# GpSimd's queue brings the second page of every pair for all eight value units of a decoder step

## The reference, cut to what matters

```python
g = x_sample                                          # (8, 4, 1024)
k_past = gather_pages(cache_k[l], page_table)         # 8 samples x 8 pages of (128, 8 heads, 64)
v_past = gather_pages(cache_v[l], page_table)
y_ssd, new_conv, new_ssm = ssd_branch(z, xbc, dt_raw, conv_state, ssm_state, ...)
    # ... y = y * silu(z); y = rmsnorm(y, norm_w)
y_att = moba_attention(q, k_all, v_all, q_start, p['rel_bias'])
h = h + jnp.concatenate([y_ssd, y_att], axis=-1) @ p['w_out'][l]
h = h + cross_attend(rmsnorm(h, p['norm_ca'][l]), mem_k, mem_v, ...)
h = h + jnp.square(jax.nn.relu(rmsnorm(h) @ p['w_up'][l])) @ p['w_down'][l]
```

## Time and profile before

| | us (share of the span) |
|---|---|
| median of three runs | 650.11 |
| the three runs | 649.38, 650.11, 651.97 |
| the profiled execution | 650.07 |
| its span, first to last instruction | 648.4 |
| PE busy | 629.1 (97%) |
| PEld busy | 504.6 (78%) |
| DVE busy | 405.7 (63%) |
| ACT busy | 152.3 (23%) |
| POOL busy | 139.0 (21%) |
| SP's and ACT's DMAs, share of the 16 engines' time | 50.9% |
| POOL's DMAs | 8.9% |

### The profile page before, as it was taken

The page is one execution under the profiler, slowest core; times in us unless marked ns, Lnnn a source line. Parts: engine busy times, 40 slices in busy tenths (PEclk is TensorE's granted clock), DMA queues, the critical chain, the costliest instruction groups (busy, mean ns, idle before and its releaser), DMA issues.

```text
span 648.4 us, 13116 instructions
## 1 busy us (share of the span) xinstructions
PE 629.1 (97%) x4877; PEld 504.6 (78%) x4877; DVE 405.7 (63%) x879; ACT 152.3 (23%) x409; POOL 139.0 (21%) x222
## 2 busy tenths in 40 slices
PE   8999999999999999999999999999999999999995
PEld 6766776676676655557667876899999999999995
DVE  3466576997764667777423346887887874553733
ACT  3110020001212875783102333211211110000001
POOL 6152212110220026151001100433443540000000
PEclk9999999999999999999999999999999999999998
DMA  8798998897942158878696551344544535534501
GB/s 311 242 295 258 290 295 262 243 289 243 286 134 66 66 194 249 311 184 248 199 324 233 210 194 66 112 149 131 171 155 138 187 132 183 176 131 150 172 5 74
DMA packets 98779, 125.75 MB, mean 194 GB/s; under 512 B 6571, under 2 KB 74687, under 8 KB 98722
## 3 DMA queue, kind: packets, MB, share of 16 engines
q1 hardware_dynamic: 92818, 106.62, 50.9%
q0 software_dynamic: 5648, 18.14, 8.9%
q10 hardware_dynamic: 256, 0.20, 0.1%
HBM read 116.64 MB, written 8.31 MB: 193 GB/s over the span
## 4 chain that ended last, share of the span: by engine, by line
PE 77%; DVE 3%; ACT 1%; issue 1%; DVEq 0%; ACTq 0%
PE ps L1618 34%; PE ps L1194 25%; PE ps L1151 4%; PE ps L1261 3%; PE ps L1427 1%; PE ps L1214 1%; PE ps L1373 1%; PE ps L1309 1%; PE ps L1157 1%; PE ps L1303 1%; PE ps L1285 1%; PE ps L1417 1%; PE ps L1406 1%; PE ps L1236 1%; PE ps L1292 1%
## 5 line engine op out<-in xcount | busy, mean ns | idle before, releaser
L1194 PE MATMUL ps<-hw,wring 128*128 128x288 f32 x576 | 148.4, 413 | 0.4 <-DVE big L2126 0.4
L1194 PEld LDWEIGHTS ps<-hw,wring 128*128 128x128 f32 x576 | 108.1, 192 | 37.3 <-issue 6.9
L2253 DVE STREAM_TRANSPOSE tmp<-big 128x1024 f32<-128x1024 f32 x32 | 37.9, 1222 | 2.5 <-PE ps L1214 2.4
L1005 POOL TENSOR_TENSOR acc<-acc,sq 128x288 f32<-128x288 f32 (+1 forms) x35 | 29.3, 836 | 31.5 <-ACT sq L1842 29.3
L2099 DVE COPY tmp<-ps 128x512 f32<-128x512 f32 (+6 forms) x35 | 21.5, 619 | 21.3 <-PE ps L1151 16.0
L1618 PE MATMUL ps<-hw,wring 128*128 128x144 f32 x256 | 34.2, 287 | 0.0
L1618 PE MATMUL ps<-big,wring 128*128 128x144 f32 x256 | 34.0, 286 | 0.0
L1618 PEld LDWEIGHTS ps<-hw,wring 128*128 128x128 f32 x256 | 32.5, 190 | 0.4 <-DVE hw L2103 0.4
L1194 PE MATMUL ps<-big,wring 128*128 128x288 f32 x128 | 32.7, 409 | 0.0
L1194 PE MATMUL ps<-attT,wring 128*128 128x288 f32 x128 | 31.9, 407 | 0.7 <-DVE hT L2148 0.7
L1618 PEld LDWEIGHTS ps<-big,wring 128*128 128x128 f32 x256 | 32.4, 190 | 0.0
(11 more groups left out here) (352 smaller groups left out, 1150.9 us busy)
## 6 DMA issues: line engine op xcount, KB each, us to landing
wring<-in_w_in SPq DMA_DIRECT2D x16, 1024.0 KB, 7.1
wring<-in_w_up SPq DMA_DIRECT2D x16, 1024.0 KB, 5.1
wring<-in_w_down SPq DMA_DIRECT2D x16, 1024.0 KB, 4.7
big<-in_cache_v SPq DMA_DIRECT2D x56, 256.0 KB, 3.5
big<-in_cache_k SPq DMA_DIRECT2D x36, 256.0 KB, 3.5
big<-in_cache_k POOLq DMA_DIRECT2D x28, 256.0 KB, 4.2
wring<-in_w_out SPq DMA_DIRECT2D x6, 1024.0 KB, 5.8
wring<-in_w_ca_kv SPq DMA_DIRECT2D x4, 1024.0 KB, 8.2
```

The lines of the kernel that those rows point to most:

```text
L1005: pool.tensor_tensor(a, a, sq[:, m % 2, 0:n], ALU.add).then_inc(acc_done, 1)
L1194: last = pe.matmul(ps[:, BANK[key], 0:width], w, rhs, start=(k == 0), stop=(k == K_TILES[kind] - 1))
L2253: dve.transpose(KT_[:, step_ % 2].rearrange("p c (w j) -> p w c j", j=32), src[:, :, :, m, :])\
```

## The change

All eight V units become shared: SP issues the first page of each pair, POOL the second. `KV_POOL` and `KV_DMAS` follow from `SHARED`, and so do the counts that PE waits for (`kv_ready`). So 24 transfers of 256 KB (six units of four) move from SP's program to POOL's. They stand at the same items of `SEQ`: at `sums 0` (V,0,2), at `seg 0 1` (V,0,3), at `unit V 0 2` (V,1,0), at `unit V 0 3` (V,1,1), at `unit V 1 0` (V,1,2), at `unit V 1 1` (V,1,3). Each is preceded by POOL's own `slot_free`, for the store of the states in the first two cases and for `v_used` in the other four.

```diff
-SHARED = [n > 0 and u[0] == "K" or u in (("V", 0, 0), ("V", 0, 1)) for n, u in enumerate(UNITS)]
+SHARED = [n > 0 and u[0] == "K" or u[0] == "V" for n, u in enumerate(UNITS)]
@@ @block.gpsimd, the loop over SEQ @@
                         load_pages(pool, n, NPAGE // 2, NPAGE, kv_pool)
                     else:
                         load_values(pool, n, 1, kv_pool)
+                elif s[0] == "unit" and s[1] == "V" and UNITS[UNIT[s[1:]] + 2][0] == "V":
+                    n = UNIT[s[1:]] + 2
+                    slot_free(pool, n)
+                    load_values(pool, n, 1, kv_pool)
+                elif s == ("sums", 0) or s == ("seg", 0, 1):
+                    n = UNIT[("V", 0, 2 if s[0] == "sums" else 3)]
+                    slot_free(pool, n)
+                    load_values(pool, n, 1, kv_pool)
                 elif s[0] == "ks" and s[3] == 1:
```

## The result

The changed kernel takes 659.61 us (median of six, 656.68 to 661.76), the kernel before 649.75 beside it. The ratio is 1.0145, with an interval of 1.0113 to 1.0178: slower by 9.4 us by the ratio (the medians differ by 9.9), where 4.6 were forecast. Its executions stand in two groups, three from 656.7 to 657.6 and three at 661.7. The loss is thus 7 to 10 us. 654.7 was too low, and the range, up to 657.2, too.

What follows compares the result with a forecast made beforehand. PE was taken as the bound, waiting for no page, with POOL's sum of squares on the edge of the path. 650.07 plus 4.6 us for the delayed adds, all else nothing, gave 654.7 us; range 652.2 to 657.2.

Steps and rivals of the forecast that it cites:

- What bounds the kernel: Whole kernel: PE is busy 97% and waits for no page; POOL's sum of squares for the SSD norm has almost no room.
- The price of a block: POOL's four page issues at a pace of 1.55 us take 6.63 us from the slot's release.
- Blocks 1 and 2: At `sums 0` and `seg 0 1`: the store freeing `sq` goes out 12.4 us later; no loss taken.
- The second rival: Store of keys slower than 10 us, ACT's squares start after 278; each us beyond is lost, 655.7 for one; chance 0.08.
- Block 3: At `unit V 0 2`: four issues for (V,1,0) delay POOL's adds of squares; PE loses 4.6 us, bounds 4.1 and 5.2.
- Blocks 4 to 6: Issues behind the adds: biases at worst 1.5 to 2.1 us late but covered; nothing taken; failed cover 656.2, chance 0.04.
- The first rival: PE's pause from 283.95 to 288.6 lowers TensorE's clock; about one dense tile at half speed, 2 us more, 656.7; chance 0.16.
- The third rival: POOL's four issues at `unit V 0 2` follow at 0.54 us; PE loses 1.7 us, 651.8, no measurable change; chance 0.14.

Runs made afterwards that it cites:

- the clock held: Changed kernel with 19 matmuls of ones on PE ahead of its wait for the SSD norm's sum of squares: 655.50 us, ratio 1.0075.
- The run without block 3: Changed kernel, but SP issues all eight pages of unit (V,1,0), the other five blocks staying with POOL: 650.32 us, ratio 1.0021.
- second measurement: The changed kernel itself measured once more, with nothing altered: 658.19 us, ratio 1.0115.
- block 3 alone: Kernel before, with only the second pages of unit (V,1,0) moved to POOL at `unit V 0 2`: 659.15 us, ratio 1.0141.

## Why the prediction was wrong, point by point

**What bounds the kernel: right.** No page and no weight block is among the waits of PE or of its weight loads in any of the runs, and POOL's sum of squares was the place.

**The price of a block: right in kind, 0.6 short.** From the slot's release (273.16) to the copy 7.2 us, forecast 6.63. The pace was 1.57, 2.04 and 1.57 us, not 1.55 three times. The copy and the adds behind it took 7.0 us where the forecast had 7.3, which gave half of that back.

**Blocks 1 and 2: no cost, as taken.** Block 1 went more slowly, at 3.00, 3.30 and 1.72 us an issue, and took 8.6 us instead of 6.2. The store that frees `sq` went out at 266.77 and landed in 3.8 us, before ACT's first square at 270.77. The second rival did not come here. It was near: in the second profiled execution of the changed kernel the store took 5.1 us and ACT's first square waited 0.7 us for it, at no loss, as the distance is 15.53.

**Block 3: right.** POOL's adds followed each other at 6.43 / 7 = 0.92 (0.955 forecast), and the pause was 4.71 (4.7 from the forecast times), in part because the two small errors above went against each other. With the clock held, the cost of the wait is 4.26 us, for which the sum had 4.6 and a lower bound of 4.1.

**Blocks 4 to 6: nothing, as taken.** The run without block 3 has all the others.

**The clock: the step that failed.** The first rival was given 0.16 and 2 us. It was no rival but the second term of the sum: the clock fell in each profiled execution whose pause was over 3 us and not filled, four of four. Its price was 3.57 us and not 2, where the sum had nothing. The argument "one dense tile or so runs at half speed" took it for granted that the clock comes back within a few microseconds of PE's resuming. In the three profiled executions with the whole pause it stayed low for 10.2 us, through the short items of heads 0 and 1. The lower speed is paid on all of these, and not on one tile. Half of the time that PE works at the low level is an upper bound of the price: in the changed kernel PE was at work for the last 8.5 of the 10.2 us, which makes 4.2, and 3.57 was measured. And the argument against, that the late store might split the pause, leaned on an event that the same text took for unlikely. The Trainium skill, "TensorE: Matmul & The Clock Gate", Part 1, has the rule that an idle array is put back to 1.2 GHz and that activity releases it. By this rule, cited beside the rival, the sum would have had the term. The runs agree as to the fall (0.50 from 285.7 in the changed kernel, with PE idle from 282.73); the release came after PE had worked from 287.45 to 295.9.

With both terms, 650.07 + 4.26 + 3.57 = 657.9, against 658.19 of the second measurement, and 659.61 of the first. What the three executions at 661.7 of the first had more is not settled, as none of them was profiled. Their mean granted clock, 0.976 against 0.984, would by the arithmetic above be some 10 us more at the low level, but the second measurement has 658.2 both with 0.989 and with 0.981, so the mean does not give the time. The execution of block 3 alone at 661.74 was profiled: it had reached (V,0,3) 1.91 us later than before by its start (the low level from 8 to 18 us and a dip to 0.96 in the window 200 to 240), had 0.9 us more in the tile under the low clock, and 1.0 us more behind PE's last group. Whether that is so in the others stays open. So does why the low level lasted 10.2 us behind 4.7 and 3.4 behind 3.15.

**The third rival** was wrong for this kernel and became true by an edit: with the page numbers read first, the four issues start within 2.4 us, a pace of some 0.8, and 0.85 us of distance is lost, which the medians do not show.

## What to carry to other kernels

A DMA issued from a computing engine costs that engine's program the whole of its issue, here 1.55 us with a page number to be read, and what counts is which instruction stands behind it: move the block behind the one that another engine waits for, or read the registers ahead of the wait. When a forecast has TensorE idle for as long as here (3.15 and 4.7 us) in the middle of a kernel, put the clock's fall into the sum and not beside it, with up to half of the time that TensorE works at the low level. No version here beats the kernel before: PE never waited for SP's issuing, and the best versions only come back to it.

## What the runs showed of the hardware that was not expected

- The low level lasted 10.2 us in all three profiled executions with a pause of 4.6 to 4.7 us, with PE at work again 1.8 us after the fall in the changed kernel (287.45 against 285.7), and 0.7 us before it where block 3 alone was moved (290.46 against 291.1).
- POOL's page loads in block 1 followed each other at 3.00 and 3.30 us, against 1.55. Full DMA engines alone do not explain it: the share was 0.97 to 1.05 from 248 to 256, and block 2 went at 1.54 to 1.87 with 0.87 to 1.05 from 261 to 267. SP's issues in about the same stretch went at 13.72 / 8 = 1.7 before. The cause is open.
- Float32 matmuls of 128 columns on 128 rows, each with its own weight load, came every 0.23 us at the full clock, 9.20 us for 40, and not every 0.11.
